# Reordering the stage borders of a hybrid decoder step

## The reference, cut to what matters

```python
D_MODEL = 1024; SEQ = 1024; DEPTH = 2; DEC_BATCH = 8
D_FF = 2816; CONV_WIDTH = 3; RET_HEADS = 4

def conv_ffn(x, buf, w_in, conv_w, conv_b, w_out):
    u = x @ w_in
    a, g = u[..., :D_FF], u[..., D_FF:]
    ext = jnp.concatenate([buf.astype(a.dtype), a], axis=1)
    c = conv_b + ext[:, 0:t] * conv_w[0]
    for j in range(1, CONV_WIDTH):
        c = c + ext[:, j:j + t] * conv_w[j]
    h = jax.nn.silu(c) * g
    return h @ w_out, ext[:, t:]

def reference(...):
    for i in range(DEPTH):
        mp, ms = attention(x) if i % 2 == 0 else retention_mixer(x, ...)
        x = layer_norm(DEEPNORM_ALPHA * x + m, ln_mix_g[i], ln_mix_b[i])
        f = conv_ffn(x, ...)
        x = layer_norm(DEEPNORM_ALPHA * x + f, ln_ffn_g[i], ln_ffn_b[i])
```

## Time and profile before

| | us |
|---|---|
| median of 3 runs (lowest, highest) | 2839.55 (2836.59, 2839.56) |
| the profiled execution's own time | 2836.83 |
| its span | 2835.0 |
| PE busy in it | 2723.2 |
| DVE, ACT, POOL busy | 1603.2, 1043.5, 775.7 |

### The profile page before, as it was taken

The page is one execution under the profiler, slowest core; times in us unless marked ns, Lnnn a source line. Parts: engine busy times, 40 slices in busy tenths (PEclk is TensorE's granted clock), DMA queues, the critical chain, the costliest instruction groups (busy, mean ns, idle before and its releaser), DMA issues.

```text
span 2835.0 us, 47487 instructions
## 1 busy us (share of the span) xinstructions
PE 2723.2 (96%) x19166; PEld 2612.8 (92%) x19166; DVE 1603.2 (57%) x3000; ACT 1043.5 (37%) x1934; POOL 775.7 (27%) x568
## 2 busy tenths in 40 slices
PE   8999987999999999998999999999988999999997
PEld 7888877999999999998999999999988999999997
DVE  6556577667675335614446354465777666664345
ACT  5445454333333122422343433422263343332123
POOL 3334351222322223402213222112222323222231
PEclk9999989999999999999999999999999999999999
DMA  4210110222224232234566565777401222223321
GB/s 136 80 47 17 31 32 32 81 76 83 75 86 136 78 120 66 77 107 137 183 194 191 187 190 192 219 252 228 150 25 65 74 85 77 81 90 123 102 71 60
DMA packets 218409, 307.27 MB, mean 108 GB/s; under 512 B 30608, under 2 KB 171536, under 8 KB 218160
## 3 DMA queue, kind: packets, MB, share of 16 engines
q1 hardware_dynamic: 153296, 242.73, 26.8%
q10 hardware_dynamic: 64896, 61.50, 6.3%
HBM read 214.81 MB, written 91.45 MB: 108 GB/s over the span
## 4 chain that ended last, share of the span: by engine, by line
PE 87%; DVE 6%; ACT 2%; issue 2%; DMA 1%; POOL 1%; SPq 0%; ACTq 0%; POOLq 0%; DVEq 0%
PE bank L664 18%; PE bank L666 17%; PE bank L665 17%; PE bank L954 9%; PE bank L956 9%; PE bank L955 9%; PE bank L818 1%; ACT y L1296 1%; PE bank L797 1%; DMA h_in<-scratch_h 1%; DVE wl L1801 1%; PE bank L1189 1%; PE bank L1142 1%; PE bank L808 1%; PE bank L718 1%
## 5 line engine op out<-in xcount | busy, mean ns | idle before, releaser
L1801 DVE TENSOR_TENSOR wl<-raw,wh 128x512 fp32r<-128x512 f32 (+1 forms) x383 | 372.4, 978 | 400.9 <-ACT wh L1257 397.0
L664 PE MATMUL bank<-xh,wh 128*128 128x344 f32 x1680 | 548.0, 326 | 16.6 <-ACT f_ab L1450 12.0
L666 PE MATMUL bank<-xh,wl 128*128 128x344 f32 x1680 | 538.5, 321 | 0.0
L665 PE MATMUL bank<-xl,wh 128*128 128x344 f32 x1680 | 537.8, 320 | 0.0
L1257 ACT ACTIVATE wh<-raw 128x512 fp32r<-128x512 f32 (+1 forms) x412 | 307.2, 764 | 338.9 <-PE bank L666 205.8
L954 PE MATMUL bank<-xh,wh 128*128 128x258 f32 x1280 | 362.9, 284 | 7.5 <-DVE f_g L2113 5.6
L1829 DVE TENSOR_TENSOR y<-bank,y 128x344 f32<-128x344 f32 x384 | 193.6, 513 | 299.7 <-PE bank L666 298.6
L956 PE MATMUL bank<-xh,wl 128*128 128x258 f32 x1280 | 362.5, 283 | 0.0
L955 PE MATMUL bank<-xl,wh 128*128 128x258 f32 x1280 | 361.9, 283 | 0.0
L664 PEld LDWEIGHTS bank<-xh,wh 128*128 128x128 f32 x1680 | 317.7, 189 | 32.1 <-ACT f_ab L1450 12.5
L665 PEld LDWEIGHTS bank<-xl,wh 128*128 128x128 f32 x1680 | 317.3, 189 | 4.8
(11 more groups left out here) (294 smaller groups left out, 6204.2 us busy)
## 6 DMA issues: line engine op xcount, KB each, us to landing
raw<-in_w SPq DMA_DIRECT2D x216, 512.0 KB, 3.8
scratch_h<-f_g SPq DMA_DIRECT2D x40, 516.0 KB, 2.7
h_in<-scratch_h SPq DMA_DIRECT2D x30, 688.0 KB, 5.2
scratch_qkvg<-p_plain ACTq DMA_DIRECT2D x96, 172.0 KB, 3.0
r_s<-in_state_in SPq DMA_DIRECT2D x32, 512.0 KB, 3.8
out_state_s<-r_s ACTq DMA_DIRECT2D x32, 512.0 KB, 5.1
scratch_qkvg<-p_rot ACTq DMA_DIRECT2D x24, 344.0 KB, 2.9
xh<-scratch_heads_hi SPq DMA_DIRECT2D x12, 688.0 KB, 8.1
```

The lines of the kernel that those rows point to most:

```text
L664: pe.matmul(out, ah, bh, start=(k == 0), stop=False)
L665: pe.matmul(out, ah, bl, start=False, stop=False)
L666: mm = pe.matmul(out, al, bh, start=False, stop=(k == n - 1))
L1801: dve.tensor_tensor(lo, source, hi.bitcast(F32), ALU.subtract).then_inc(S["lo_done"], 1)
```

## The change

It touches five places. (1) Both borders into the up projections: layer 0's first three jobs are done by halves with `var` after the second half has begun; chunks 1 and 2 take the `a` sides first, two jobs by halves; g sides keep banks 3 and 5; the orders of ACT and DVE follow; products of pair 2 are interleaved over `sub`; the first weight sums come earlier, since their source unit is split by POOL and four units have other slots; `xt_lo` of two of the four x operands goes from DVE to POOL. (2) The last pair does products 4 and 6 last, and its convolution and gate come ahead of the down jobs on DVE. (3) In the down projections two loads of h and then the store of the last pair come before a weight load. (4) In retention SP issues `queries(0)`, `values(0)` ahead of the last four weight loads. (5) In block 4 of layer 1 the two `mean`s come two jobs later and the four splits for `fin` come at jobs 9, 11, 13, 15 instead of 18, 20, 22, 23.

```diff
@@ tables
-                units.append((n + 2 * BATCH + 2 * p + which, half, (start + 7 * p + i) % 8,
+                at = 7 * p + i
+                units.append((n + 2 * BATCH + 2 * p + which, half, early + at if at < 4 else (start + at) % 8,
-            b = ((2, 3, 4, 5), (2, 3, 4, 2), (3, 2, 3, 2))[ch][2 * t + which]
+            b = 2 + 2 * t + which
-            b = key[3] % 6
+            b = (1, 3, 2, 5, 6, 7)[key[3]] if key[2] == 0 and key[3] < 6 else key[3] % 6
+def pair_order(t):
+    if t == BATCH:
+        return [(sub, n) for n in range(2, 7) for sub in range(2)]
+    if t == FT - 1:
+        return [(sub, n) for sub in range(2) for n in (0, 1, 2, 3, 5)] + [(sub, n) for n in (4, 6) for sub in range(2)]
+    return [(sub, n) for sub in range(2) for n in range(7)]
@@ tensor engine, ffn_batch
+        if L == 0:
+            halves(tiles[:3], 0, 0)
+            halves(tiles[:1], 0, 1)
+            var(u + 1)
+            halves(tiles[1:3], 0, 1)
+            mean(u + 2)
+        else:
+            pe.wait_ge(S["n_lo"], 2 * u + 2)
+            var(u + 1)
+            ffn_up(L, 0, 0, 0)
+            ffn_up(L, 0, 1, 0)
+            mean(u + 2)
+            ffn_up(L, 1, 0, 0)
+        ffn_up(L, 1, 1, 0)
...
+        for ch in (1, 2):
+            tiles = batch_tiles(ch)
+            halves(tiles[:2], ch, 0)
+            if ch == 1:
                 var(u + 2)
+            halves(tiles[:2], ch, 1)
+            for t, kind in tiles[2:]:
+                ffn_up(L, t, kind, ch)
@@ vector engine, ffn, from chunk 2's normal_lo on
+        normal_lo(u + 2, (0,))
+        xt_raw(L, 0)
+        normal_lo(u + 2, (1,))
+        xt_raw(L, 1)
+        split_next(pair_unit(L, BATCH, 4) - split[0])
+        conv(L, 1, 1)
+        xt_raw(L, 2)
         gate(L, 0, 1)
+        xt_lo(L, 0)
         gate(L, 1, 1)
         conv(L, 0, 2)
+        split_next(2)
+        conv(L, 1, 2)
         gate(L, 0, 2)
         gate(L, 1, 2)
@@ gpsimd
+        weight_sums(L, BATCH)
+        xt_lo(L, 1)
+        xt_lo(L, 2)
@@ vector engine, down jobs
+            mean_free = L == 1 and b == N_DOWN - 2
-                if b and q in (18, 20, 22, 23):
+                if b and q in ((9, 11, 13, 15) if mean_free else (18, 20, 22, 23)):
                     split_next(1)
@@ tensor engine, down jobs
-                if L == 1 and b == N_DOWN - 2 and q in (KT + 5, 2 * KT + 5):
+                if L == 1 and b == N_DOWN - 2 and q in (2 * KT - 1, 3 * KT - 1):
                     mean(u + 3 if q < 2 * KT else u + 4)
@@ sync engine
-        pair_out(L, FT - 1)
+                if b == 1 and ch == 1:
+                    pair_out(L, FT - 1)
+                    slabs_to(s + 2 * FT + 4 * b + 1)
...
-    slabs_to(due_by(J["p", 0, 11, 2]) + RAW)
+    slabs_to(due_by(J["p", 0, 7, 2]) + RAW)
     queries(0)
     values(0)
+    slabs_to(due_by(J["p", 0, 11, 2]) + RAW)
```

More of the change, by code:

```diff
@@ L71, in up_jobs @@
     for ch in range(NCH):
[L72 to L77, removed]
+        out += [("up", L, t, kind, ch) for t, kind in batch_tiles(ch)]
+        if ch != 1:
+            out += [("sp", L, BATCH, ch // 2, n) for n in range(2)]
+    return out + [("sp", L, t, sub, n) for t in range(BATCH, FT) for sub, n in pair_order(t)]
 def down_tiles(b):
@@ L135, in unit_table, with ffn @@
         n += 5
-    def ffn(L, n, slots, start):
+    def ffn(L, n, slots, early, start):
         u0 = len(units)
@@ L198, in lo_table @@
 def lo_table():
-    mine = set(range(5, 26)) | {U_R + j for j in range(2, 6)} | {U_F1 + j for j in range(2, 6)}
+    mine = set(range(5, 27)) | {U_R + j for j in range(2, 6)} | {U_F1 + j for j in range(2, 7)}
     on_pool, nth, seen = [], [], [0, 0]
@@ L959, in ffn_batch, with halves @@
     def ffn_batch(L, u):
[L961 to L965, removed]
+        def halves(tiles, ch, half):
+            pe.wait_ge(S["n_lo"], 2 * (u + ch) + half + 1)
+            for t, kind in tiles:
                 s = (S_F0 if L == 0 else S_F1) + 2 * t + kind
-                if half == 0:
+                if ch == 0 and half == 0:
@@ L968, in ffn_batch @@
                     wait_slab(pe, S, s)
[L969 to L979, removed]
+                up_half(("up", L, t, kind, ch), s, ch, half)
@@ L1041, in ffn @@
         ffn_batch(L, u)
[L1042 to L1045, removed]
+        for t in range(BATCH, FT):
+            for sub, n in pair_order(t):
+                product(L, t, sub, n)
         for b in range(N_DOWN - 1):
@@ L1467, in copied @@
             after(act, S["keep"], L * FT + t - 1)
+        if n in (2, 4) and t == BATCH:
+            act.wait_ge(S["jobs"], J["sp", L, t, 1, n])
         if n == 2 and sub == 0:
@@ L2168, in ffn_pair @@
         end = t == FT - 1
-        if t > BATCH:
-            for step in range(3):
-                pair_conv(L, t - 1, step)
+        if t == BATCH:
+            combine(L, t, 0, 0)
+            combine(L, t, 1, 0)
+            split_next(3)
+            combine(L, t, 0, 1)
+            combine(L, t, 1, 1)
+            split_next(3)
+            for sub in range(2):
+                combine(L, t, sub, 2)
+                combine(L, t, sub, 3)
+            split_next(1)
+            return
+        for step in range(3):
+            pair_conv(L, t - 1, step)
         combine(L, t, 0, 0)
-        if t > BATCH:
-            pair_gate(L, t - 1)
+        pair_gate(L, t - 1)
         combine(L, t, 0, 1)
-        if t == BATCH:
-            split_next(3)
+        if t < FT - 1:
+            split_next(1)
+            combine(L, t, 0, 2)
+            combine(L, t, 0, 3)
+            split_next(2)
             combine(L, t, 1, 0)
@@ L2181, in ffn_pair @@
             split_next(1)
[L2182 to L2184 removed]
+            combine(L, t, 1, 2)
+            combine(L, t, 1, 3)
             return
[L2186 removed]
+        combine(L, t, 1, 0)
+        split_next(1)
+        combine(L, t, 1, 1)
+        pair_conv(L, t, 0)
+        pair_conv(L, t, 1)
         combine(L, t, 0, 2)
         combine(L, t, 0, 3)
[L2189 to L2193 removed]
+        pair_conv(L, t, 2)
         combine(L, t, 1, 2)
         combine(L, t, 1, 3)
+        split_next(1)
+        pair_gate(L, t)
     def ffn(L, u):
         dve.wait_ge(S["f_in"], 32 * (L + 1))
+        if L == 0:
+            conv(L, 0, 0)
         inverse_root(u + 1)
@@ L2489, in vector_engine @@
     x_lo(1)
-    split[0] = 26
+    split[0] = 27
     dve.wait_ge(T["turn_in"], 32)
@@ L2697, in pool_engine @@
     border(0)
+    split_lo(26)
     ffn(0)
@@ L2708, in pool_engine @@
     border(1)
-    for n in range(U_F1 + 2, U_F1 + 6):
+    for n in range(U_F1 + 2, U_F1 + 7):
         split_lo(n)
```

159 lines of the change are left out of this document (75 added, 84 removed).

## The result

The changed kernel took 2787.84 us (median of 4 runs, 2783.27 to 2789.93), the kernel before 2838.93 (4 runs, 2836.59 to 2839.56). The ratio is 0.9819 with a 95% interval of 0.9802 to 0.9836, so it is faster by 51 us, where 58 were forecast and the forecast time was 2782. The spans of the two profiled executions are 2784.6 and 2835.0 us, 50.4 apart.

The account below looks back on a forecast made before the run. TensorE, busy 2723.2 of 2835.0 us, was taken to set the time, leaving only idle time and clock to win. Gains 15 + 10 + 14 + 13 + 6 = 58 from 2839.55 gave 2781.5, taken as 2782; range 2758 to 2806.

Parts of the forecast that it names:

- Rival A: Borders and end: VectorE and POOL seldom block each other, so the gain is 80 us, time 2760; chance 0.17.
- C: Loops over pairs: they fall behind, each of 36 pairs waiting 2.0 us for a weight sum; 2854 us, chance 0.05.
- B: Down starts: waits only change releaser, loads and POOL's subtractions set the pace; that 14 us gain vanishes, 2795, chance 0.16.
- First border: Layer 0's entry to the up projections up to pair 3: idle and clock fall from 31.0 to 16.0, gain 15 us.
- Chunk 1's second half waits for its `n_lo` 1.7: First border: TensorE waits 1.7 us for the norm's low half, behind VectorE's two normal_lo halves and xt_raw.
- the two POOL blocks: Borders: POOL's xt_lo subtractions hold up VectorE; in the first, gate(1,1) comes 3.0 us late and gate(1,2) 5.4.
- Second border: Layer 1's entry to the up projections: of 24 us to win, 13 idle and 1.5 clock remain; gain 10 us.
- Down starts: Last pair and start of the down projections: earlier gate and loads gain 7 us per layer, 14 together.
- All that follows shifts 7 to 8, more than the 4.3 + 1.0: Down starts: earlier gate and loads shift what follows by 7 to 8 us, covering block 1's waits of 4.3 and 1.0.
- Retention: Start of retention: the 11.47 us wait and 2.2 of clock go, 0.6 remains for the next load; gain 13 us.
- The end: Last down blocks of layer 1: fin's 5.3 us wait and 1.5 of clock go, mean still waits; gain 6 us.
- The term of the mean: The end: mean comes two jobs (7.5 us) later, POOL's sums some 7 to 8 later; a wait of 3.3 us left.

Follow-up runs that it names:

- e2: Changed kernel with xt_lo(1) and xt_lo(2) back on VectorE behind chunk 2's last gate, none on POOL; 2779.09 us, ratio 0.9793.
- e1: Changed kernel with layer 0's convolution of tile 0's first chunk moved behind chunk 1's inverse root and chunk 2's centring; 2782.10 us, ratio 0.9797.
- e8: Changed kernel with the edits of e1, e2 and e3, plus VectorE's and ScalarE's orders around pair 2 changed; 2762.15 us, ratio 0.9737.
- e3: Changed kernel with VectorE's two splits of the first down block at jobs 7 and 8 instead of both at 11; 2781.95 us, ratio 0.9797.
- e9: Changed kernel with SyncE's old order at the down starts: last pair's store, weight load, then loads of h; 2785.94 us, ratio 0.9822.
- e5: Kernel before with the fourth part alone (queries and values ahead of the last four weight loads); 2825.69 us, ratio 0.9962.
- e12: The changed kernel unaltered, run once more on the chip of the last experiments; 2788.97 us, ratio 0.9828.

## Why the prediction was right, and which terms were off

- **The mechanism held in the main.** The loops over pairs are full in both kernels (380.00 of 380.00 us), all 50 us come from idle time and clock at the five places, and no new wait is above 6 us. Rival A is refuted by the stretched rows and by e2, C by the full loops. B came in part: the down starts gained, but what remains there goes back to POOL's subtractions for h. Two of the signs named beforehand failed: the first border's window is 89.6 with a clock of 0.92 (84 and 0.95 or more were named), and waits over 1 us stand in the down starts.
- **First border, 15 forecast, 9.8 measured.** The failed step is "Chunk 1's second half waits for its `n_lo` 1.7". I replayed VectorE's queue with durations only and missed what its first instruction there waits for: the memset on POOL. Measured 5.59 and a slow stretch of 6.8 us; e1 takes 4.6 of it out. The idle time came near the forecast all the same, 15.1 against 13.8, and that is luck: the two POOL blocks, forecast at 3.0 and 5.4, cost 2.90 and 3.22 (e2 shows them to be POOL's). The rest of the shortfall is clock. The full-clock work of this border is 69.8 us (busy in e8's window at clock 1.00) and not 68.4, so 1.4 less was to be won, and the clock left is 74.5 - 69.8 = 4.8 where 2.2 was forecast. The part came out just below my lower bound of 10.
- **Second border, 10 and 10.5.** The number is right by two errors that cancel. The idle time left is 82.95 - 72.67 = 10.3 where 13 was forecast, and the clock left is 72.67 - 69.08 = 3.6 (69.08 is busy in e8's window) where 1.5 was. Here the convolution stands behind the root, and no wait for `n_lo` came. Waits for gates 2.90 and 3.03, pair 3 1.64.
- **Down starts, 14 and 8.0.** The failed step is "All that follows shifts 7 to 8, more than the 4.3 + 1.0". The gate did come 7 us earlier, but the wait fell from 4.34 to 2.06 only, as the adds stand behind two splits that POOL holds up. I had used exclusion for the borders and not here. e3 and e9 show its price, 2.0 and 2.2 us in layer 0, and e9 that the part I counted on ("SP issues two loads at once") gains nothing.
- **Retention, 13 and 12.8.** Wait 1.02 where 0.6 was forecast, clock 1.00 where it was 0.50. e5 alone gives 11.4 us with an interval of 4 either side.
- **The end, 6 and 9.3.** `fin` waits for nothing, as forecast. The term of the mean was off twice: a job of that block has 12 matmuls, so two jobs are 3.8 us and not 7.5, and the splits lengthened the sums by 1.8, where 7 to 8 were put on them and on later adds. 1.40 of wait was left and not 3.3, and the slow stretch behind it went too. This part isn't steady: in e12 the wait is 4.16. The sums took 8.97 us there and not 8.02, and began 1.8 us later against TensorE, behind POOL's last subtraction for h. From the start of this wait to the end of the span it is 88.4 us in e12 and 83.7 in the first profile, so with e12's wait the part is worth about 4.6.
- **The sum** was 58 against 51 by medians: two terms were too high by 5.2 and 6.0, one too low by 3.3.

## What to carry to other kernels

A replay of queues needs each instruction's wait beside its duration: one cheap step here waited for a memset in another engine's full queue and held a whole norm's chain, which cost 4.6 us. When work goes from VectorE to GpSimd, count what its instructions do to VectorE's small ones at that very place, and where adds or gates stand behind. An earlier load is no gain by itself: what it sets off can collide with something that was free before. And a forecast that comes out right in its sum can still be wrong in its terms, as in the second border: compare idle time and clock one by one.

## What the runs showed of the hardware

VectorE and GpSimd did not share in these places, they took turns by instruction. Between two 4.6 us subtractions of GpSimd one VectorE instruction got through; with GpSimd's work in quarters every VectorE step of the convolution, even a copy of 128x10 (0.17 us alone, 1.24 here), lasted 1.0 to 1.6 us, about one quarter. VectorE's gates, which read one operand from PSUM, kept their 0.50 us in between. So here the cut of GpSimd's instruction helped a long VectorE instruction (3.26 us instead of 6.61) and hurt a row of small ones (7.9 instead of 6.1).
